# Small transfers of the state-space layer and the attention issued by GpSimd instead of SyncE, rows of powers split by group, two output blocks stored by ScalarE

## What is computed

```
proj = x @ w_in                      # q, k, v (8 heads x 128), u (64 groups x 16), two gates
y_att = neighbourhood_attention(q, k, v, rpb) @ w_na_out
y_s  = s5(u, forward) + s5(u, backward) + d * u     # complex diagonal state space, 64 states a group
y_s  = gelu(y_s);  y_s = y_s * sigmoid(y_s @ w_glu + b_glu)
mix  = (sig(g_att) * y_att + sig(g_ssm) * (y_s @ w_s5_out)) @ w_out
h    = LN(alpha * x + mix)
out  = LN(alpha * h + (silu(h @ w_gate) * (h @ w_up)) @ w_down)
```

## Time and profile before

| | |
|---|---|
| median of 3 runs | 1401.08 us (1400.88 to 1401.15) |
| the profiled execution's own time | 1401.64 us |
| its span, first to last instruction | 1399.8 us |
| TensorE busy | 1378.1 us, 98% |
| VectorE busy | 948.8 us, 68% |
| ScalarE busy | 689.1 us, 49% |
| GpSimd busy | 82.9 us, 6% |
| mean granted TensorE clock | 0.997 of full speed |

### The profile page before, as it was taken

The page is one execution under the profiler, slowest core; times in us unless marked ns, Lnnn a source line. Parts: engine busy times, 40 slices in busy tenths (PEclk is TensorE's granted clock), DMA queues, the critical chain, the costliest instruction groups (busy, mean ns, idle before and its releaser), DMA issues.

```text
span 1399.8 us, 23670 instructions
## 1 busy us (share of the span) xinstructions
PE 1378.1 (98%) x9116; PEld 1184.0 (85%) x9116; DVE 948.8 (68%) x1297; ACT 689.1 (49%) x978; POOL 82.9 (6%) x88
## 2 busy tenths in 40 slices
PE   8998999999999999999999999999999999999998
PEld 7877888888888888887888888888888888888886
DVE  7977999999985789567555555555555554545454
ACT  5443555555456775336554445444554543333332
POOL 1800000000000000000122220000000000000001
PEclk9999999999999999999999999999999999999999
DMA  8767666666655686663666666666766666666663
GB/s 296 213 195 229 207 204 204 184 213 214 185 159 167 196 273 223 195 194 114 203 186 190 185 189 189 185 189 186 229 184 190 186 193 194 189 193 194 192 196 105
DMA packets 92402, 273.44 MB, mean 195 GB/s; under 512 B 14242, under 2 KB 25250, under 8 KB 91940
## 3 DMA queue, kind: packets, MB, share of 16 engines
q1 hardware_dynamic: 88788, 268.99, 62.0%
q10 hardware_dynamic: 3536, 3.38, 0.7%
HBM read 267.01 MB, written 5.31 MB: 195 GB/s over the span
## 4 chain that ended last, share of the span: by engine, by line
PE 90%; DVE 5%; DMA 2%; SPq 1%; issue 1%; ACT 0%; DVEq 0%; ACTq 0%
PE bank L1601 41%; PE bank L1603 21%; PE bank L1615 8%; PE bank L1616 8%; PE bank L1617 8%; DVE wlo L972 2%; PE bank L1713 1%; PE bank L1691 1%; DMA lrow<-lam_dram 1%; DMA raw<-wstream 1%; DVE scratch L998 1%; DVE scratch L995 1%; PE bank L1671 1%; PE bank L1891 0%; SPq L340 0%
## 5 line engine op out<-in xcount | busy, mean ns | idle before, releaser
L972 DVE TENSOR_TENSOR wlo<-raw,whi 128x1024 fp32r<-128x1024 f32 x463 | 567.2, 1225 | 318.4 <-ACT whi L569 314.8
L569 ACT ACTIVATE whi<-raw 128x1024 fp32r<-128x1024 f32 x463 | 489.4, 1059 | 472.4 <-PE bank L1603 246.6
L1601 PE MATMUL bank<-act,whi 128*128 128x512 f32 x2304 | 585.2, 395 | 10.3 <-DVE wlo L972 7.0
L1601 PEld LDWEIGHTS bank<-act,whi 128*128 128x128 f32 x2304 | 414.2, 189 | 90.7 <-DVE wlo L972 6.9
L1603 PEld LDWEIGHTS bank<-act,wlo 128*128 128x128 f32 x2304 | 314.6, 190 | 22.8
L1603 PE MATMUL bank<-act,wlo 128*128 128x256 f32 x2304 | 321.3, 282 | 0.0
L1615 PE MATMUL bank<-whi,mid 128*128 128x512 f32 x352 | 136.9, 389 | 0.0
L1616 PE MATMUL bank<-wlo,mid 128*128 128x512 f32 x352 | 136.9, 389 | 0.0
L1617 PE MATMUL bank<-whi,mid 128*128 128x512 f32 x352 | 136.9, 389 | 0.0
L1615 PE MATMUL bank<-whi,act 128*128 128x512 f32 x192 | 75.8, 395 | 3.4 <-DVE wlo L972 3.4
L1617 PEld LDWEIGHTS bank<-whi,mid 128*128 128x128 f32 x352 | 66.1, 188 | 13.8
(11 more groups left out here) (180 smaller groups left out, 1067.4 us busy)
## 6 DMA issues: line engine op xcount, KB each, us to landing
raw<-wstream SPq DMA_DIRECT2D x463, 512.0 KB, 3.7
bt<-b_rows SPq DMA_DIRECT2D x8, 512.0 KB, 5.7
lrow<-lam_dram SPq DMA_DIRECT2D x48, 64.0 KB
lnrow<-lnrows SPq DMA_DIRECT2D x3, 1024.0 KB, 6.8
xraw<-xT SPq DMA_DIRECT2D x8, 256.0 KB, 5.6
bs<-b_states SPq DMA_DIRECT2D x8, 256.0 KB, 5.2
tb<-lag_dram SPq DMA_DIRECT2D x32, 64.0 KB, 3.5
hp<-xtok SPq DMA_DIRECT2D x4, 512.0 KB, 4.6
```

The source lines that it names most:

```text
L569: act.activation(whi[:, c % SPL, :], raw[:, c % RAW, :], ACT.Copy).then_inc(hi_ready, 1)
L972: dve.tensor_tensor(wlo[:, c % SPL, :], raw[:, c % RAW, :], whi[:, c % SPL, :].bitcast(F32), ALU.subtract).then_inc(lo_ready, 1)
L1601: pe.matmul(bank[:, :], whi[:, s, i * P:(i + 1) * P], both, start=start and i == 0, stop=stop and i == kn - 1)
```

## The change

Every small transfer that SyncE issued for the state-space layer and the attention is issued by GpSimd instead. SyncE keeps the weights, x, `cols`, the tokens and the LayerNorm rows. GpSimd's program gets them in this order: after x has landed, `cn` of tiles 0 and 1, `bt` 0, `bs` 0 and `bm` 0 and 1 (six transfers); then its table of rotations as before; then the six stores of `store_lam`, the rows of tile 0, `u4` of tile 0, and a loop over the heads. A step of `stage_rows` becomes two transfers, one for each half of the partitions (16 rows of 2 KB each), so a tile's rows are 12 transfers of 32 KB instead of 6 of 64 KB. In the tail ScalarE stores the two blocks that GpSimd finishes, and SyncE the other seven transfers in the order in which VectorE finishes them.

```diff
 (SyncE: for c in range(RAW, H_LOOP) and for f, j in the loop: only load(0, ...) is left)
-                if c in (24, 25, 26):
-                    store_lam(c - 23)
-                if c == 28:
-                    sp.wait_ge(rows_set, 2)
-                    sp.wait_ge(lam_stored, 96)
-                if c in (28, 29):
-                    for k in range(3 * (c - 28), 3 * (c - 28) + 3):
-                        stage_rows(0, k)
...
-                    if f == 0 and j == 1:
-                        sp.wait_ge(bp_prod, 2)
-                        stage_bt(1)
...
-                row = lam_dram[n - 1, 2 * f + d, :, :, :].rearrange("g (o q) n -> g o (q n)", o=1)
-                sp.dma_start(lrow[j::Q, d, :, :, :].rearrange("p q r n -> p (q r n)"),
-                             row.to_broadcast([2, GC, 512])).then_inc(lrow_staged, 16)
+                for g in range(2):
+                    row = lam_dram[n - 1, 2 * f + d, g:g + 1, :, :].rearrange("o q n -> o (q n)")
+                    pool.dma_start(lrow[64 * g + j:64 * g + 64:Q, d, :, :, :].rearrange("p q r n -> p (q r n)"),
+                                   row.to_broadcast([GC, 512])).then_inc(lrow_staged, 16)
...
+            pool.wait_ge(x_landed[XP - 1], 16)
+            for f in range(2):
+                stage_c(f)
+            stage_bt(0)
+            stage_bs(0)
+            for f in range(2):
+                stage_bias(f)
 (GpSimd's table of rotations)
+            for n in range(1, Q):
+                store_lam(n)
+            pool.wait_ge(rows_set, 2)
+            pool.wait_ge(lam_stored, 96)
+            for k in range(6):
+                stage_rows(0, k)
+            pool.wait_ge(u_stored, 16 * KS)
+            stage_u(0)
+            for f in range(HEADS):
+                if f == 0:
+                    pool.wait_ge(bp_prod, 2)
+                    stage_bt(1)
+                    for k in range(6):
+                        stage_rows(1, k)
+                if f < KS - 1:
+                    if f > 0:
+                        pool.wait_ge(y_done, 2 * f - 1)
+                    stage_u(f + 1)
+                    pool.wait_ge(w_round, f + 1)
+                    stage_bs(f + 1)
+                stage_tb(f)
+                if f + 2 < KS:
+                    pool.wait_ge(bp_prod, 2 * f + 4)
+                    stage_bt(f + 2)
+                    for k in range(6):
+                        stage_rows(f + 2, k)
+                    pool.wait_ge(c_prod, 4 * f + 4)
+                    stage_c(f + 2)
+                if 1 <= f < HEADS - 1:
+                    pool.wait_ge(att_lo, f)
+                    stage_bias(f + 1)
+                    stage_v(f + 1)
 (ScalarE, at its end)
+            for n, i in enumerate(LN2_POOL):
+                t, b = i // 4, slice(i % 4 * 512, i % 4 * 512 + 512)
+                act.wait_ge(ln2_pool, n + 1)
+                act.dma_start(out[t * P:(t + 1) * P, b], hp[:, t, b]).then_inc(pool_stored, 16)
```

More of the change, by code:

```diff
@@ L98 @@
 LN2_BANKS = (0, 1, 2, 3, 6, 7)
-LN2_STORES = [0, 3, 1, 2, 7, 4, 5, 6]
 U_EVAC = [i + LAG for i, (_, h) in enumerate(U_ORDER) if h == 1]
@@ L219, in build @@
         v_staged = [sem("v_staged0"), sem("v_staged1")]
+        v_later = [sem("v_later0"), sem("v_later1")]
         bias_staged = [sem("bias_staged0"), sem("bias_staged1")]
@@ L458, in _ @@
                 load(0, c)
[L459 to L463, removed]
+            for n, i in enumerate(LN2_DVE):
+                sp.wait_ge(ln2_dve, n + 1)
                 t, b = i // 4, slice(i % 4 * 512, i % 4 * 512 + (256 if i == LN2_DVE[5] else 512))
@@ L468, in _ @@
             sp.dma_start(out[t * P:(t + 1) * P, b], hp[:, t, b]).then_inc(stored, 16)
-            sp.wait_ge(stored, 16 * len(LN2_STORES) + 16)
+            sp.wait_ge(stored, 16 * len(LN2_DVE) + 16)
+            sp.wait_ge(pool_stored, 16 * len(LN2_POOL))
         @block.gpsimd
@@ L484, in _, with stage_u, stage_c @@
             pool.memset(lnm[:, :, 7:8], 1.0).then_inc(ones_ready, 1)
+            def stage_u(f):
+                for j in range(Q):
+                    pool.dma_start(u4[j::Q, f % 2, :, :], u_dram[:, f, NB * j:NB * j + NB]
+                                 .rearrange("(q r) c -> r q c", r=32)).then_inc(u4_staged[f % 2], 16)
+            def stage_c(f):
+                pool.dma_start(cn[:, f % 2, :, :, :].rearrange("p r t n -> p (r t n)"), c_rows[:, f, :]
+                             ).then_inc(bc_staged[f % 2], 16)
@@ new lines, in stage_bias, with stage_v, stage_tb @@
+            def stage_bias(f):
+                pool.dma_start(bm[:, f % 2, :, :], bias[f, :, :].rearrange("p (t n) -> p t n", t=TT)
+                             ).then_inc(bias_staged[f % 2], 16)
+            def stage_v(f):
+                pool.dma_start(vcur[:, f % 2, :, :], v_dram[:, DH * f:DH * f + DH].rearrange("(t p) n -> p t n", p=P)
+                             ).then_inc(v_later[f % 2], 16)
+            def stage_tb(f):
+                pool.wait_ge(lags_stored, 16 * f + 16)
+                if f > 0:
+                    pool.wait_ge(y_done, 2 * f - 1)
+                for j in range(Q):
+                    o = 32 * (Q - 1 - j)
+                    pool.dma_start(tb[j::Q, :, :, :].rearrange("p q j n -> p q (j n)"),
+                                 lag_dram[:, o:o + P].rearrange("(q r) m -> r q m", r=32)).then_inc(tb_staged, 16)
@@ new lines, in store_lam @@
+            def store_lam(n):
+                pool.wait_ge(lam_kept, 2)
+                o = (n - 1) % 2 * GROUPS
+                for g in range(2):
+                    pool.dma_start(lam_dram[n - 1, :, g, :, :],
+                                 lamT[o:o + GROUPS, (n - 1) // 2, g, :, :].rearrange("p r n -> p (r n)")).then_inc(lam_stored, 16)
+            pool.wait_ge(x_landed[XP - 1], 16)
[3 more added lines that the diff above has]
+            stage_bs(0)
@@ L1140, in form_b @@
                     dve.wait_ge(rows_set, 2)
-                    dve.wait_ge(lrow_staged, 96 * f + 96)
+                    dve.wait_ge(lrow_staged, 192 * f + 192)
                     dve.wait_ge(c_formed, max(2, 2 * f))
@@ L1738, in attend @@
                 pe.wait_ge(pt_ready, f + 1)
-                pe.wait_ge(v_staged[f % 2], 16 * (f // 2) + 16)
+                if f < 2:
+                    pe.wait_ge(v_staged[f], 16)
+                else:
+                    pe.wait_ge(v_later[f % 2], 16 * (f // 2))
                 for b in range(TT):
```

86 lines of the change are left out of this document (13 added, 73 removed).

## The result

The changed kernel takes 1392.45 us (median of 4 runs, 1392.12 to 1394.41) against 1401.12 us before on the same chip (4 runs, 1400.88 to 1401.36): 8.7 us less, a ratio of 0.9941 [0.9924, 0.9958]. That is faster by 0.59%, more than the 0.2% of the prediction's bound. The profiled execution itself took 1392.12 us, its span is 1390.1 us (before 1399.8); it is the fastest of the four and the one before stands above its median, so the spans differ by 9.7 us where the medians differ by 8.7. Two executions further down fell into a slower state of the chip with a lower granted clock, one of e5 (1584.28 us) and one of the kernel before beside e5 to e8 (1939.87 us), and no ratio counts them.

A forecast was written before the change was run, and what follows sets the result against it. About 11.6 us could be won at 92.8 to 135.2 us, where TensorE waits for VectorE and VectorE for rows. The mark's 2.4 us plus the tail's 1.4 made 3.8 us, forecast 1397.3 us, range 1389.5 to 1411.

The forecast's parts named there:

- the mark: Start of VectorE's product of tile 1, 112.03 us before; each us earlier or later moves the end by the same.
- c: Time GpSimd spends issuing one transfer, taken as 0.8 us; break-even at 0.88, bounds 0.52 and 1.25 us.
- rival B: GpSimd's queue takes the place of the slow rows, c from 1.01 to 1.7: 1408.2 us at c = 1.15; chance 0.27.
- A: GpSimd's issue takes about as long as breaks even, c from 0.83 to 1.01: 1401.0 us; chance 0.20.
- the formula's floor: Earliest start of VectorE's product of tile 0, 90.7 us, however soon its rows land; holds at c = 0.52.
- M: Forecast start of VectorE's product of tile 1: 84.85 + 31c for c above 0.62, 109.65 us at c = 0.8.
- the landings: Time from a group's last issue until its transfers have landed, for stores and rows: 3.0 us each, bounds 2.6 to 3.9.
- Rival E: Rows crawl as before because the memory side is slow, not the spread: 1413.1 us; C, D and E together 0.09.
- ScalarE's waits: ScalarE's 19.8 us of waits for late chunks, at 92.8 to 135.2 us, were to be nearly gone.
- the early transfers: Six transfers (`cn`, `bt`, `bs`, `bm`) moved to GpSimd behind x: costed at 0, 5 us without cover.
- rival C: GpSimd's queue is late in every head, c above 1.7: about 1451 us at 1.9; C, D and E together 0.09.
- rival D: VectorE slows down beside GpSimd; at 20%, 31 us over eight heads, about 1428 us; C, D and E together 0.09.

The follow-up runs named there:

- e5: Changed kernel with whole rows of 64 KB from GpSimd's queue and its descriptor scratch doubled (2048 instead of 1024): 1391.66 us, ratio 0.9933 to the kernel before.
- e8: Kernel before with rows as 12 transfers of 32 KB on SyncE's queue, each half of a row for both groups, led by 2: 1402.7 us, ratio 1.0011.
- e9: Changed kernel with 6 of tile 1's 12 row halves issued from SyncE's queue instead of GpSimd's: 1389.48 us, ratio 0.9923 to the kernel before.
- e4: Changed kernel with a tile's rows in 24 transfers of 16 KB (8 rows) instead of 12 halves: 1400.94 us, ratio 0.9995 to the kernel before.
- e2: Kernel before with only the rows cut into 12 halves of 32 KB, still on SyncE's queue: 1394.69 us, ratio 0.9952 to the kernel before.
- e6: Kernel before with the row halves and the tail's stores, everything else still on SyncE's queue: 1392.89 us, ratio 0.9941 to the kernel before.
- e3: Kernel before with the tail alone, GpSimd's two output blocks stored from ScalarE's queue: 1399.94 us, ratio 0.9990 to the kernel before.
- e7: Changed kernel with SyncE issuing the stores of the powers and, for tiles 0 and 1, group 1's row halves: 1391.5 us, ratio 0.9927 to the kernel before.
- e1: Changed kernel with a tile's rows as 6 whole transfers of 64 KB from GpSimd's queue: 1400.42 us, ratio 0.9992 to the kernel before.

## Why the prediction was right, and what of it was not

**Right: the place and the mark.** One for one was the claim, and it held: the product of tile 1 came 8.57 us earlier, chunk j = 5 8.57 us earlier, and the span fell by this and the tail's 1.13 us. e9 and e4 repeat it in both directions, e4 with 9.6 us at the mark and 9.5 in the span, e9 with 3.0 and 2.3, where almost nothing of the idle time was left to win.

**Luck in the number.** The gain was forecast as 3.8 us and is 8.7, more than twice that; 1397.3 us was the forecast, 1392.45 the time. That it lies within the stated 1389.5 to 1411 us is owed to the width of the range, whose low end stands for c = 0.52, and to two errors that partly cancel, the next two.

**Mis-sized: c.** The term c was taken as 0.8 us and is 0.48, even under the 0.52 that I had put as its lower bound. The failed step is "rounded down from the middle": GpSimd's products beside a busy VectorE were no measure for an issue, as rival B's own counter-argument said (an issue reads no operand), and the row of SyncE's issues was the nearer of the two. The excess of the gain comes from this, and rivals A and B, which both needed c above 0.83, are off with it: with c = 0.48 the formula's floor holds and gives M = 90.7 + 2.35 + 6.2 + 3.0 = 102.3 us; measured were 103.46. That the measured c is under the lower bound, the mark not, is the second error's doing.

**Mis-sized the other way: the landings and the gaps.** The prediction's 3.0 us run from the end of the last issue. Measured like that, the landings are 2.95 (stores), 4.50 (rows of tile 0) and 3.60 us (tile 1). The median of tile 0's twelve is 3.0 us even from an issue's start, but the product waits for the last of them, and that is the slowest (5.0 from its start). The sum also has no term for two gaps: 0.68 us from the end of VectorE's products to GpSimd's first issue, and 0.17 us from the last landing to VectorE's start. At tile 1 this makes 0.60 + 0.68 + 0.17 = 1.45 us more than the formula, and product 0 started 0.33 us before the formula's floor, which leaves 1.12 of the 1.16 us between 102.3 and 103.46. The floor itself was too high: VectorE was ready at 89.78 us instead of 90.7, and the 0.59 us of wait there are for rows.

**Right: the rows crawled for their leading 2, not for the memory side.** Rival E is off: the median landing of the halves in tile 0 is 3.0 us, and e2 against e8 shows the cause. What the prediction did not see is that the crawl belongs to SyncE's queue and is much weaker on GpSimd's (e5).

**Came true for another reason: ScalarE's waits.** They fell from 19.8 to 2.4 us, as forecast, and chunk loads issued in 81 to 110 us land in 5.3 us at the median instead of 9.3 (4 were forecast). The prediction put both down to the rows' spread. The landing is (4.6 us in e2), but the waits are not: with the same halves on SyncE's queue they are 23.3 us. They fell since nothing stands ahead of the chunks in SyncE's queue any more, and they are no sign of the gain, for e6 has 22.9 us of them and the changed kernel's ratio.

**Right: the loop, the early transfers, the tail.** From 157.6 to 405.9 us TensorE is busy in 248.30 of 248.30 us, so rival C is off. In the first 56 us it is busy in 52.33 instead of 52.09 us, so the six transfers moved there cost nothing. The tail was priced at 1.4 and gave 1.13 in the span, 1.3 in e3 by itself.

**Off: rival D.** VectorE's low halves take 1216 ns at the median in 100 to 400 us beside GpSimd's issues, and took 1217 ns before.

**What the change as a whole was.** The prediction costed the new queue and the halves as one thing. Taken apart they are: halves 6.6 us (e2), tail 1.3 us (e3), new queue 0 to 0.9 us once the halves are there (e6). The parts don't simply add: on GpSimd's queue with twice the room the halves are worth nothing (e5). The queue's own use is that its waits hold up no chunk (e7), and its price is 25 issues a head which lie beside other work.

**What stays open.** From which transfer on GpSimd pauses wasn't worked out from its room and the packets. Whether chunks land sooner beside GpSimd's whole rows because these go to other engines or because they have their own DMA queue is not shown. e9 with e5's room and whole rows wasn't tried.

## What to carry to other kernels

When a small transfer lands late, or large ones beside it do, look at its leading dimension before its size or its queue: on SyncE's queue the same bytes in the same number of transfers took 7.6 us more when each was led by a 2 instead of a 16 (e8 against e2). Once it spreads, the issues between a buffer's release and its next use are the price, some 0.5 us each on either queue, so split only as far as the spread needs, and share them over two queues only where the second has no wait ahead of loads that others need. Undo the parts of a change one at a time: here the largest part of the diff, the new queue, was worth next to nothing beside the halves, and two small edits made the gain. And check such a part against the other one too: whole rows on the new queue lost the gain only for want of room for descriptors.

## What the runs showed of the hardware that I had not expected

- GpSimd's issue of a plain transfer is quick and steady: 0.48 us for 16 rows of 2 KB (481 to 521 ns over 96 issues beside a busy VectorE), 0.50 for 8 rows, 0.55 for the 128 rows of `bt`, 0.61 for 32 rows of 2 KB led by 2 (e1, e5). SyncE took 0.52 for the last and 0.59 for the first.
- GpSimd's queue stands still for up to 7 us at a time when its room for descriptors is small (e1, five pauses of 17.1 us in all before rows in 74 to 131 us), and doubling that room is worth 8.3 us in an otherwise equal kernel (e5).
- A transfer led by 2 behaves differently by queue: chunks beside it land in 9.3 us when it is issued by SyncE and in 5.1 us when by GpSimd (e5). From SyncE about 2 of its packets are in flight at a time, whatever their size (2.1 before with 2 KB, 2.2 in e8 with 1 KB); led by 16, up to 16 are (e2).
